# Six joins of a two-layer decoder step: four sums of squares in place of five, placed behind block 6, and a new order on ScalarE at the end of each phase

## The reference, cut to what matters

```python
hp = hp + _rmsnorm(mp, norm_mix_post[layer])
hp = hp + _rmsnorm(_swiglu(_rmsnorm(hp, norm_ffn_pre[layer]), w_ffn_gate_up[layer], w_ffn_down[layer]), norm_ffn_post[layer])
# _rmsnorm: y = x32 * rsqrt(mean(x32 * x32, axis=-1) + EPS) * g
```

## Time and profile before

| | |
|---|---|
| median of 3 runs | 2754.19 us (2754.17 to 2757.58) |
| profiled execution: time, span | 2752.42 us, 2750.2 us |
| mean granted TensorE clock | 0.969 of 2.4 GHz |
| busy: PE, PEld | 94%, 84% of the span |
| busy: DVE, ACT, POOL | 47%, 37%, 44% |
| chain that ended last | PE 77%, DVE 6%, ACT 3% |

### The profile page before, as it was taken

How to read it: one execution, slowest core, us unless ns; L and a number is a source line. 1 busy time by engine, 2 the same in 40 slices (tenths; PEclk the granted TensorE clock), 3 DMA queues, 4 the chain that set the end, 5 groups by cost and what they waited for, 6 DMA issues and landing times.

```text
span 2750.2 us, 43876 instructions
## 1 busy us (share of the span) xinstructions
PE 2594.5 (94%) x15403; PEld 2312.8 (84%) x15407; DVE 1285.0 (47%) x1779; ACT 1028.9 (37%) x1516; POOL 1212.7 (44%) x608
## 2 busy tenths in 40 slices
PE   6979859999999999999978899999999999999999
PEld 4769547788887787888867599999999999999999
DVE  4467777796887454303456433211234253220234
ACT  4545743432324434323246434222224435222222
POOL 4444243554554335545545224444444334443442
PEclk9989879999999999999989999999999999999999
DMA  6445011233332222333331211232232221232232
GB/s 163 115 103 145 16 58 54 69 100 91 99 101 72 87 82 71 101 91 99 101 109 35 85 55 54 84 92 70 83 89 73 76 72 49 83 91 73 81 90 75
DMA packets 447742, 229.45 MB, mean 83 GB/s; under 512 B 86460, under 2 KB 439440, under 8 KB 447127
## 3 DMA queue, kind: packets, MB, share of 16 engines
q1 hardware_dynamic: 447647, 228.21, 29.1%
HBM read 212.84 MB, written 15.43 MB: 83 GB/s over the span
## 4 chain that ended last, share of the span: by engine, by line
PE 77%; DVE 6%; ACT 3%; issue 2%; POOL 1%; DVEq 0%; POOLq 0%; ACTq 0%
PE psum L714 65%; PE psum L748 2%; PE psum L822 1%; PE psum L992 1%; PE psum L1084 1%; PE psum L1069 1%; DVE probs_t L2374 1%; DVE scores L2112 1%; DVE top L2105 1%; PE psum L1092 1%; DVE row_stats L2365 1%; PE psum L848 1%; PE psum L1194 1%; ACT act_split L1710 0%; PE psum L1141 0%
## 5 line engine op out<-in xcount | busy, mean ns | idle before, releaser
L1856 POOL TENSOR_TENSOR w_lo<-w_raw,w_hi 128x1024 fp32r<-128x1024 f32 (+1 forms) x334 | 854.6, 2559 | 1248.0 <-ACT w_hi L1335 1247.9
L714 PE MATMUL psum<-act_split,w_hi 128*128 128x288 f32 (+1 forms) x6096 | 1344.1, 329 | 11.4 <-POOL w_lo L1856 4.9
L714 PEld LDWEIGHTS psum<-act_split,w_hi 128*128 128x128 f32 x6096 | 980.7, 189 | 97.7 <-issue 5.9
L1335 ACT ACTIVATE w_hi<-w_raw 128x1024 fp32r<-128x1024 f32 (+1 forms) x334 | 375.0, 1124 | 1288.2 <-PE psum L714 1263.4
L714 PE MATMUL psum<-act_split,w_lo 128*128 128x288 f32 (+1 forms) x3048 | 832.4, 328 | 0.0
L714 PEld LDWEIGHTS psum<-act_split,w_lo 128*128 128x128 f32 x3048 | 519.6, 189 | 39.7
L714 PE MATMUL psum<-hidden_split,w_hi 128*128 128x288 f32 (+1 forms) x2112 | 461.8, 327 | 0.0
L714 PEld LDWEIGHTS psum<-hidden_split,w_hi 128*128 128x128 f32 x2112 | 339.5, 189 | 27.3
L714 PE MATMUL psum<-hidden_split,w_lo 128*128 128x288 f32 (+1 forms) x1056 | 287.9, 327 | 0.0
L2433 DVE TENSOR_TENSOR temps<-psum,root_of_input 128x512 f32<-128x512 f32 (+1 forms) x88 | 63.4, 721 | 358.2 <-PE psum L714 343.5
L2439 DVE TENSOR_TENSOR temps<-psum,temps 128x512 f32<-128x512 f32 (+1 forms) x88 | 63.3, 719 | 357.4 <-PE psum L714 332.4
(11 more groups left out here) (296 smaller groups left out, 2327.6 us busy)
## 6 DMA issues: line engine op xcount, KB each, us to landing
w_raw<-in_w_ffn_gate_up SPq DMA_DIRECT2D x352, 256.0 KB, 3.1
w_raw<-in_w_ffn_down SPq DMA_DIRECT2D x64, 384.0 KB, 3.7
w_raw<-in_w_ffn_down SPq DMA_DIRECT2D x64, 320.0 KB, 4.1
w_raw<-in_w_in_odd SPq DMA_DIRECT2D x64, 256.0 KB, 3.0
w_raw<-in_w_in_even SPq DMA_DIRECT2D x60, 256.0 KB, 3.9
w_raw<-in_w_out_odd SPq DMA_DIRECT2D x32, 256.0 KB, 3.0
x_rows<-in_x_prompt SPq DMA_DIRECT2D x8, 512.0 KB, 6.1
w_raw<-in_w_out_even SPq DMA_DIRECT2D x32, 128.0 KB, 2.8
```

Source lines behind the costliest of these rows:

```text
L714: mm = pe.matmul(PS[:, 2 * p + b, 0:hi - lo], w[:, p, at], x(k)[:, lo:hi], start=(k == 0 and w is WH and x is x_hi), stop=(k == ph.kt - 1 ...
L1335: act.activation(WH[:, p, 0:n], WR[:, p, 0:n], ACT.Copy).then_inc(S("w_hi"), 1)
L1856: pool.tensor_tensor(WL[:, p, 0:n], WR[:, p, 0:n], WH[:, p, 0:n].bitcast(F32), ALU.subtract).then_inc(S("w_lo"), 1)
```

## The change

- Squares: blocks 0 to 3 are now added by VectorE into one tile (three sums, after blocks 3, 4 and 6), and blocks 4 and 5 into another (a fourth sum, after block 7). In g=0 squares 1, 2, 3 and 5 lie in PSUM, in g=1 all lie in SBUF (`TT`, `SS`).
- TensorE adds four tiles in place of five: the first at k=6, then block 6, the pair (4,5) and block 7 at k=7. The semaphore by which ScalarE waited for TensorE's sums is gone.
- `spread` stands ahead of the second chunk's last two blocks instead of ahead of its last one.
- In `loop`, the last round's `take` for p=1 stands ahead of the next phase's high part for p=1.

```diff
--- before.py
+++ after.py
@@ -342,15 +342,15 @@
         ROW_BANK = (6, 4)
         LAST_BANK = (4, 0, 2, 6, 4)
 
-        def even_square(n, g):
-            return SQ[:, n // 2 % 2, 0:T[g]]
-
-        def odd_square(n, g):
-            if g or n == NB - 1:
-                return TT[:, n // 2 % 2, 0:T[g]]
-            return PS[:, (5, 3)[n // 2 % 2], :]
-
-        PAIRS = 3
+        def square(n, g):
+
+            if n in (0, 4):
+                return SQ[:, n // 4, 0:T[g]]
+            if g == 0 and n in (1, 2, 3, 5):
+                return PS[:, (5, 3, 1, 5)[(1, 2, 3, 5).index(n)], :]
+            return (SS[:, 0:T[g]], TT[:, 0, 0:T[g]], TT[:, 1, 0:T[g]])[(3, 1, 2).index(n % 4)]
+
+        ADDS = ((1, 0), (2, 0), (3, 0), (5, 4))
 
         def norm_at(kind, g, s):
             if kind == "load":
@@ -752,18 +752,19 @@
 
                 def squares(k):
 
-                    if m is None or k not in (3, 5, 6, 7):
+                    if m is None or k < NB - 2:
                         return
-                    if k == 3:
+                    if k == NB - 2:
+                        pe.wait_ge(S("sq_two"), 4 * m + 3)
                         open_sums()
-                    if k < NB - 1:
-                        j = (3, 5, 6).index(k)
-                        pe.wait_ge(S("sq_two"), PAIRS * m + j + 1)
-                        add_sums(even_square(2 * j, g), g).then_inc(S("sq_used"), 1)
+                        add_sums(square(0, g), g)
                         return
-                    for n in (NB - 2, NB - 1):
-                        pe.wait_ge(S("sq_m"), 8 * m + n + 1)
-                        add_sums(odd_square(n, g) if n % 2 else even_square(n, g), g)
+                    pe.wait_ge(S("sq_m"), 8 * m + 7)
+                    add_sums(square(6, g), g)
+                    pe.wait_ge(S("sq_two"), 4 * m + 4)
+                    add_sums(square(4, g), g)
+                    pe.wait_ge(S("sq_m"), 8 * m + 8)
+                    add_sums(square(7, g), g)
                     close_sums().then_inc(S("n_sum"), 1)
 
                 first, second = ((WH, a_hi), (WL, a_hi)), ((WH, a_lo),)
@@ -778,7 +779,7 @@
 
                 for p in (0, 1):
                     for k in (ph.kt - 2, ph.kt - 1):
-                        if m is not None and p and k == ph.kt - 1:
+                        if m is not None and p and k == ph.kt - 2:
                             spread(root_at, g)
                         if p == 0:
                             pe.wait_ge(S("a_hi"), 8 * split + k + 1)
@@ -1344,9 +1345,11 @@
                             pass
                         elif not last:
                             hi_part(ph, i + 1, p)
-                        elif ph.next:
+                        elif ph.next and p == 0:
                             hi_part(ph.next, 0, p)
                         take(i, p)
+                        if last and ph.next and p:
+                            hi_part(ph.next, 0, p)
                 if early:
                     body(0, False, True)
                 if unrolled:
@@ -1709,11 +1712,9 @@
                     act.wait_ge(S("x_new"), 8 * (4 * g + s) + n + 1)
                     act.activation(AR[:, 0, n, 0:T[g]], X[:, n, 0:T[g]], ACT.Identity, scale=gain(base, layer, n)).then_inc(S("a_hi"), 1)
                     act.activation(Y[:, n, 0:T[g]], X[:, n, 0:T[g]], ACT.Identity, scale=gain(base, layer, n)).then_inc(S("z_in"), 1)
-                    if n in (4, 6):
-                        act.wait_ge(S("sq_used"), PAIRS * m + n // 2 - 1)
-                    if n in (5, 7):
-                        act.wait_ge(S("sq_two"), PAIRS * m + n // 2 - 1)
-                    act.activation(odd_square(n, g) if n % 2 else even_square(n, g), X[:, n, 0:T[g]], ACT.Square).then_inc(S("sq_m"), 1)
+                    if n >= 5:
+                        act.wait_ge(S("sq_two"), 4 * m + n - 4)
+                    act.activation(square(n, g), X[:, n, 0:T[g]], ACT.Square).then_inc(S("sq_m"), 1)
                 root(r_at(g, SPRE[s]), g)
                 nxt = (phase("gu", g), phase("v", g), phase("gu", g, 1))[s]
                 act.wait_ge(S("w_used"), nxt.c0 + 1)
@@ -2499,10 +2500,13 @@
                     dve.wait_ge(S("x_t"), q + n + 1)
                     dve.scalar_tensor_tensor(out=hv(X[:, n, 0:T[g]], g), in0=scaled(g), scalar=gain(base, layer, n),
                                              in1=hv(X[:, n, 0:T[g]], g), op0=ALU.mult, op1=ALU.add).then_inc(S("x_new"), 1)
-                    if s < 3 and n in (3, 5, 7):
-                        dve.wait_ge(S("sq_m"), 8 * (3 * g + s) + n - 1)
-                        two = even_square(n - 3, g)
-                        dve.tensor_tensor(two, odd_square(n - 2, g), two, ALU.add).then_inc(S("sq_two"), 1)
+                    if s < 3 and n in (3, 4, 6, 7):
+                        other, into = ADDS[(3, 4, 6, 7).index(n)]
+                        dve.wait_ge(S("sq_m"), 8 * (3 * g + s) + other + 1)
+                        if other in (2, 3):
+                            dve.wait_ge(S("sq_two"), 4 * (3 * g + s) + other - 1)
+                        two = square(into, g)
+                        dve.tensor_tensor(two, square(other, g), two, ALU.add).then_inc(S("sq_two"), 1)
                 if s == 3:
                     return
                 inverse(r_at(g, SPRE[s]), g)
```

## The result

The changed kernel takes 2763.78 us (median of 14 runs, 2752.66 to 2789.32) against 2754.46 of the kernel before beside it (14 runs): ratio 1.0057, 95% interval 1.0038 to 1.0075. The ratio is one of means, and the highest of the 14 pull it up; the medians are 9.3 us apart. The forecast was no change, 2755.8 us with a range up to 2763: the median of all 14 lies just outside, on the slow side.

What follows compares the result with a forecast made beforehand. TensorE, busy 94% of the span, was taken to bound the kernel. Terms -0.3 - 2.7 + 1.4 + 0.8 + 0.6 + 0.2 + 0.5 + 0.3 + 0.8 = +1.6 us gave a 2755.8 us median, range 2748.5 to 2763.

Steps and rivals of the forecast that it cites:

- The clock: Six joins at 0.50 (1.2 GHz): +1.4 us for the two that kept 1.00, +0.8 for the other four.
- The third rival: Joins: clock falls early in the tail, stays down to the next chunk; 6.4 on top, 2762.2 us; chance 0.19.
- Its own sign: Joins, deciding point of the third rival: the clock is down before the first group behind block 7.
- Four groups: Sums in the joins, four groups for five: gain 0 in g=0, -0.1 a join in g=1; -0.3 us for three.
- the fourth rival: g=1 joins: three VectorE sums ahead of block 7, each 0.8 longer by the port; 4.8 on top, 2760.6; chance 0.10.
- The spread: Earlier spread saves 0.9 us in each of s=1, g=0, s=0, g=1 and s=1, g=1: -2.7 us.
- the condition I gave: Joins: the spread gains at 1.2 GHz, where the path runs through it; at full clock its gain is 0.
- ScalarE's order: Down-phase ends +0.6 and +0.2, gates +0.5 and +0.3, gate-up to down +0.8 for two: ScalarE's later weights cost time.
- The first rival: Joins keep or regain the full clock: 7.9 less, with 2.4 of ScalarE's order against it; 2748.7 us; chance 0.13.
- the second: Phases using `loop`: ScalarE's new order is hidden and the joins gain as forecast; 2753.4 us; chance 0.16.

Runs made afterwards that it cites:

- e1: Only the change's four sums of squares at the end of the pass, on the kernel before; spread and ScalarE's order unchanged: 2767.54 us, ratio 1.0039.
- e13: e9 with the sum of squares 4 and 5 moved into the last block, so three sums stand in a row: 2754.17 us, ratio 0.9991.
- e8: The kernel before, unchanged, run once more for a second profile: 2756.38 us.
- e6: e1 with VectorE's four additions of squares cut to one column each: 2764.09 us, ratio 1.0043.
- e9: e1 with the first sum (squares 0 to 3) at block 5 and the second (4 and 5) at block 6: 2753.36 us, ratio 0.9997.
- e16: The whole change without ScalarE's new order (edits of e1 and e2): 2764.73 us, ratio 1.0036.
- e15: e9 with the spread moved ahead of the second chunk's last two blocks: 2756.47 us, ratio 1.0006.
- e2: Only the spread moved ahead of the second chunk's last two blocks, on the kernel before: 2756.24 us, ratio 1.0006.
- e3: Only ScalarE's order of work in `loop` changed, on the kernel before: 2755.62 us, ratio 1.0010.
- e4: The whole change again, on the same chip as its three parts: 2765.43 us, ratio 1.0044 against the kernel before.
- e5: e1 with the second chunk's products of block 6, wide matmuls, placed between the sums; no work added: 2772.4 us, ratio 1.0062.
- e12: The kernel before with one more group of one-column matmuls, never read, ahead of the closing one: 2768.72 us, ratio 1.0050.
- e14: e9 with the first sum moved from block 5 to block 6; the last block keeps two sums: 2766.87 us, ratio 1.0055.
- e11: e1 with two more groups of one-column matmuls, never read, at blocks 3 and 5: 2773.51 us, ratio 1.0090.

## Why the prediction was wrong, by its own steps

**The clock: the step that failed.** I forecast 0.50 in all six joins, and that came. What was wrong is the price, +1.4 for two joins and +0.8 for four. I let the clock fall late, so that little more than the root's way was slow. It fell while the sums still ran in s=1 and s=2, g=0 of e1 and in s=2, g=0 of the change; in s=0 of both it fell at the closing. In e1 s=2, g=0 closed its sums at 19.5 us behind the join's start, against 18.28 before, and needed 5.98 from there to the third chunk against 4.37; that is 2.8 for one join where I had 0.7. In the profile of the change itself the two joins that had kept the full clock, s=0 and s=2 of g=0, took 0.8 and 2.0 us more than before. In g=1 the clock was also down in the post norm ahead of two joins (from the opening of its sums to VectorE's first residual operation 7.61 us in place of 6.00 in e1). e1's median is 13.0 above before; 0.9 of it is the groups themselves (below), and some 12 are left for the clock, against my 2.2; what VectorE's collisions add to them is not told apart.

The third rival comes nearest, "the clock falls early in the tail and stays down". It had 0.19 and 2762.2. Its own sign did not come: in g=0 the first group behind block 7 starts about 15.9 us behind the join's start, and the earliest fall in any profile is at 17.1. The reason that I gave for it, three groups in a row, is refuted by e13. What the costly kernels have in common is four groups from block 6 on, and that is the step I priced wrong: such a tail lost the clock in all 30 joins of g=0, in 17 of them ahead of the closing; with three groups it fell in 9 of 24, in 2 ahead of the closing. The kernel before was no firm base either: I took s=0 as a join that keeps 1.00, and e8 loses it there.

**Four groups.** In g=0 I had a gain of 0; where the clock held, the sums closed 18.54 us behind the start (s=1, after) and not 18.28: +0.25 each. In g=1 I had -0.1; in s=0, where the clock falls 20.5 us behind the start in either kernel, they closed at 22.09 and 22.04: +0.05. Together +0.9 for -0.3. The reason fits too: in e6, without VectorE's long sums, the same join closes at 21.50, so the collisions ate the half microsecond that the change frees. The Trainium skill (SBUF — State Buffer, Who interferes with whom) says that a VectorE operation with two SBUF inputs contends with a GpSimd one that reads SBUF; the rows agree, 2.03 beside 0.75. As for the fourth rival, it had 4.8 on top of my sum; all collisions together are worth 3.4 us in the medians (e6 against e1), which the ratios don't tell from nothing, and part of it may come by way of the clock. In e9 collisions lengthen three splits in each join of g=1 to 1.75, 2.04 and 1.97 us, and the sums of s=0 still close at 21.99, against 22.04 before.

**The spread.** -2.7 was right inside the change. In the three joins of the term, s=1, g=0 and s=0 and s=1 of g=1, the way from the closing to the third chunk is 1.1, 0.7 and 0.9 us shorter in e16 than in e1, 2.7 together. Each against its own before, e1's median is +13.0 and e16's +9.0, but by the ratios they are only 0.8 apart. Where the clock is low, closing to third chunk becomes 4.73 for 5.60 (s=0, g=0, e9 and e15). That was the condition I gave, and alone the move gives nothing (e2, e15). In e15 the joins of g=0 took 68.7 us against 71.0 in e9, but those of g=1 91.1 against 87.5; e2, with the same move, has 91.2 there. Whether the move causes that loss is open, as e8 shows the same 34.7 us in s=2, g=1 without it.

**ScalarE's order.** +2.4 in five places. In the profiles: gate-up to down +1.0 (forecast 0.8), s=3, g=0 +0.44 (0.6), s=1, g=1 +0.04 (0.2), gate of g=0 +0.6 (0.5) and of g=1 +0.4 (0.3), the last two e4 against e16. In the medians 1.0 (e3) and 1.9 (e4 against e16, each against its own before), neither told from nothing. The size was right in the profiles; by it the order is some fifth of the loss.

The first rival is refuted by the joins, the second by the stalls just named.

**What stays open.** Which property of the tail the clock follows: the number of groups from block 6 on sorts the profiles, but no run shows why. In s=2, g=0, e5 spreads its sums over nearly the same time as e13 (5.1 and 5.4 us from opening to closing) and has wide matmuls between them, yet it loses the clock and e13 does not. No kernel tried is faster than before: e13 has the best ratio, 0.9991, and its interval, 0.9976 to 1.0005, takes in 1.

## What to carry to other kernels

Where an engine fills its waiting time with small work, don't take that work out and hang it behind the last arrival to save an instruction group: what was free becomes part of the critical tail, and in this kernel the clock then multiplied it: 0.9 us of longer sums became some 13. Ask of each piece when it can start, and start it one step before the last data. And when a total doesn't move, check that the long stretches which the edit doesn't touch took the same time in both profiles, and count the clock over several profiles.

## What the runs showed of the hardware that was not expected

**Two steady rates at one granted clock.** In g=1, where a matmul has 288 columns, TensorE's records start 133.3 ns apart on average in nearly all of the long phases, but 130.0 in three stretches (after from 1690 to 2085, e12 in the same stretch, e14 behind its last join), constant through the stretch and with the clock at 1.00. (The expectations speak of 131.6 and 128.2; from start to start over windows of 40 and 50 us it is 133.3 and 130.0.) Over one stretch of 410 us the faster rate is worth 10 us, more than the change. Single executions of before at 2742 to 2748 us would fit it; none was profiled. The cause is open.

**A long low stretch.** 7 of the 26 executions of the whole change and 2 of 6 of e11 took 2784 us or more, none of the kernel before. The profile of e4 is one of them. Its windows of the attention of g=1, and then those of e1:

```profile
1560.00:1600.00 40.00, 40.00 (x131) 21.53 (x131) 9.52 (x25) 10.64 (x28) 0.00 (x0) 0.50 0.38 109
```

```profile
1560.00:1600.00 40.00, 36.29 (x200) 22.03 (x200) 13.40 (x34) 16.38 (x49) 0.00 (x0) 0.88 0.40 116
```

In e4 the clock stays at 1.2 GHz from 1555.9 to 1624.2 us; TensorE is busy the whole 40 us of the window and does 131 matmuls where the other does 200. The stretch from the third chunk of s=2, g=0 to the next join is 616.6 us in e4 and 594.3 to 597.9 in the 17 other profiles. Nothing was run to find out why some executions fall into this.
